# Latent attention heads: one rotation of the shared key part, rotated parts turned in pairs, and two conditioning units moved from TensorE to VectorE

## The chip, the cores and the metric

The kernel runs on one core of a Trainium2 chip. Its engines are TensorE (PE: matrix products and transposes; PEld is its weight load), VectorE (DVE), ScalarE (ACT), GpSimd (POOL) and SyncE (SP, which here issues the large loads). The metric is the device time of one execution in microseconds (us), the median of several runs.

## The reference, cut to what matters

Two transformer blocks and a third, hybrid one run over 256 tokens of width 1024, in 32-bit floats. The change touches the second block's latent attention, and the row of conditioning values that the third block uses later:

```
a = h @ w_a                                  # 384 query latents, 256 key/value latents, 64 shared key values
cq, ckv, k_pe = split(a)
q  = (rms_norm(cq) @ w_qb).reshape(s, 8 heads, 192)
kv = (rms_norm(ckv) @ w_kvb).reshape(s, 8 heads, 128 + 128)
k  = concat([kv[..., :128], broadcast(k_pe over the 8 heads)])
q, k = rms_norm(q, q_gain), rms_norm(k, k_gain)          # over the 192 of a head
q, k = rope(last 64 of q), rope(last 64 of k)
o = causal_softmax(q k^T / sqrt(192)) @ v
mod = silu(c) @ w_ada + b_ada                # 1024 x 6144, in three groups of 2048 columns
```

The block's mixture of experts follows: 64 experts, of which every weight is read (three matrices of 1 MB each).

## The kernel before

Rows of 256 tokens are kept as two tiles of 128 partitions (TT = 2). Weights come in units of 1 MB or less, most into a ring of 12 slots, some into slots that lie in the large work areas A and BC. SyncE issues all these loads in one order, written out by hand; each waits for a semaphore that says that its slot was used. All other engines run one instruction list each, in the order of the stages at the end of the file.

The latent stage: `pa` multiplies the latents, `t3` turns them, `pq` makes the queries (four blocks of two heads), `pkv` the keys and values (four blocks of two heads). ScalarE drains each block (`copy_q`, `copy_kv`) and then squares it (`heads_scalar`), one item of two heads at a time. The items are `l_items`: 0 to 3 hold query heads, 4 to 7 key heads. VectorE takes them in this order (`heads_vector`): it sums the squares (L2118), rotates the last 64 values of each head with four operations, of which two have a wait for their own result behind them (L2124 to L2127), and then scales the item before with the root that GpSimd made of its sum (`heads_gpsimd`, L2092 and L2093; `scale_heads`, L2109 and L2110). The 64 shared key values are copied into all eight key heads first (L2097) and then rotated with each key item. ScalarE's first square waits for these copies.

`t4` turns the heads to have channels on the partitions: 16 fills, in the order `l_order`, four PSUM banks in turn. A fill is one head of queries or keys: two transposes of its 128 plain values and two of its 64 rotated ones (L646). ScalarE evacuates queries and the first two key heads (L658, L660), VectorE the other keys (L662, L664), in the order of the fills; a fill's bank is free for the fill four later once it is evacuated. The rotated channels lie in `peT`, on partitions 0 to 63; partitions 64 to 127 are zeroed by GpSimd (L2177), since scores multiply all 128.

The conditioning row `cond2` has eight units. The first five (`spread` = 5) are added on VectorE with one operation each (L1112, L1115), and TensorE multiplies that sum with ones; the units 5 to 7 it multiplies by themselves, into bank 3 (L1131). These products stand between the fills of `t4` (`latents_tensor`). ScalarE then copies the row and issues its store (L1139, L1141), between its fills 5 and 7. The attention's first scores (L723) and masks (L798) follow; the fills of keys 6 and 7 are evacuated between the first masks.

The next mixture's first loads into A wait for all fills to be evacuated (`rows_turned`), those after them for attention scores (`first_half_2`).

Of the kernel before, what the change touches and what calls it, by code (L numbers as in the profile page):

```python
# [8 lines left out]
ALU = mybir.AluOpType  # L9
# [5 lines left out]
P = 128  # L15
# [91 lines left out]
def build(nc, t, out):  # L107

    with ExitStack() as ctx:
# [514 lines left out]
        def turn_stage(name, ready, jobs, by=None, fill_ready=None, banks=(4, 5), signal="turn_done"):  # L624
# [25 lines left out]
            def evac(eng, scalar, first, last):  # L650
                for f, fill in enumerate(fills):
# [498 lines left out]
        cond1, cond2, cond3 = Conditioning(0, 3), Conditioning(1, 3, 5), Conditioning(2, 3)  # L1150
# [846 lines left out]
        pe_zeroed = shared("cleared", 1)  # L1997
# [13 lines left out]
        def latent_gpsimd(pool):  # L2011
            pool.wait_ge(*pe_zeroed(1))
# [81 lines left out]

        def heads_vector(dve):
            for tt in range(TT):
                nc.vector.tensor_copy(k_l[:, tt, :, NOPE:], hn[:, tt, MLA_Q + MLA_KV:A_WIDTH].unsqueeze(1)  # L2097
                                      .broadcast_to([P, HEADS, ROT])).then_inc(l_pe.sem, 1)
# [6 lines left out]
            def scale_heads(j):  # L2105
                x = l_items[j][0]
# [5 lines left out]
            for j, (x, qk, _) in enumerate(l_items):  # L2112
                dve.wait_ge(*l_sq(j + 1))
                if j == 3:
                    cond2.vector(dve, 1)
                if j >= 2:
                    dve.wait_ge(*l_rs(j - 1))
                nc.vector.tensor_reduce(l_stat(j, 68), l_squares(j).rearrange("p t h d -> p (t h) d"), AX,  # L2118
                                        ALU.add).then_inc(l_ss.sem, 1)
                cs, sn = (gtab[:, qk, k, :, :].unsqueeze(2).broadcast_to([P, TT, n, ROT]) for k in range(2))  # L2120
# [6 lines left out]
                dv.done(nc.vector.tensor_tensor(t1_, t1_, t2_, ALU.add))  # L2127
                if j >= 1:
                    scale_heads(j - 1)
            scale_heads(len(l_items) - 1)  # L2130
# [952 lines left out]
```

## Time and profile before

| | |
|---|---|
| median of 3 runs | 1501.95 us (1501.71 to 1501.95) |
| the profiled execution | 1501.71 us, of which 1500.0 us are the span of the trace |
| TensorE busy | 1301.6 us, 87% of the span |
| VectorE, ScalarE, GpSimd busy | 666.0, 273.8, 131.6 us |
| loads and stores | 513.63 MB, 342 GB/s over the span |

Times in the rows count from the start of the span. The latent stage lies at about 600 to 661 us, its attention at 660 to 696, between the streamed mixtures of the first two blocks. A row of a timeline gives the start, the duration, the engine, the line of the kernel, the operation, the tiles that it writes and reads, the count, and in brackets the time that its engine stood idle before it and what released it. Instructions of an engine overlap at their ends, so the pace of a queue is read from start to start. Matmuls are pipelined and their ends are modelled.

### The profile page before, as it was taken

Reading aid. Unit: us, or ns where it says so; the run is one execution under the profiler, and the core shown is the slowest. Engines: PE = TensorE matmul, PEld = TensorE weight load, DVE = VectorE, ACT = ScalarE, POOL = GpSimd, SP = SyncE. Lnnn points to the kernel's source line nnn. Section 1 sums busy time; section 2 is a strip of 40 time slices with the busy share of each in tenths; the row PEclk is TensorE's granted clock in tenths of the full one; section 3 lists DMA queues with packets and bytes.
Section 4 is the critical chain, followed back from the end, with each engine's and each line's share of the span. In section 5 each row is a group of like instructions: output and inputs, shape, how many; then the busy total and the mean of one; then the engine's idle time right before and its main releaser. Section 6 shows DMA issues by size and latency. Waiting matters only on the chain.

```text
span 1500.0 us, 25645 instructions
## 1 busy us (share of the span) xinstructions
PE 1301.6 (87%) x9730; PEld 806.1 (54%) x9730; DVE 666.0 (44%) x1622; ACT 273.8 (18%) x756; POOL 131.6 (9%) x201
## 2 busy tenths in 40 slices
PE   9999999766776679999999766776679999999997
PEld 4455565433443344665665433443344875899943
DVE  3874634221222123682633221122123646699976
ACT  2153211100010001362211100010000235222200
POOL 1312000000000000210100000000000133222100
PEclk9999999988898899999999898898889999999999
DMA  8979799999999999959899999999999992654400
GB/s 292 401 283 341 289 422 404 421 421 422 422 421 422 422 422 398 365 204 420 321 420 401 421 420 422 422 422 422 423 422 401 384 365 66 211 169 169 169 29 28
DMA packets 120555, 513.63 MB, mean 342 GB/s; under 512 B 12296, under 2 KB 46796, under 8 KB 69144
## 3 DMA queue, kind: packets, MB, share of 16 engines
q1 hardware_dynamic: 118576, 507.30, 84.7%
q0 software_dynamic: 1728, 5.12, 1.0%
q8 instruction: 54, 0.88, 0.2%
q14 instruction: 29, 0.24, 0.0%
q10 hardware_dynamic: 168, 0.09, 0.0%
HBM read 511.39 MB, written 1.08 MB: 342 GB/s over the span
## 4 chain that ended last, share of the span: by engine, by line
PE 58%; DMA 19%; SPq 17%; issue 3%; DVE 2%; ACT 1%; ACTq 0%; POOL 0%; POOLq 0%; DVEq 0%
DMA ring<-in_moe_w_up 15%; SPq L1872 13%; PE bank L1415 9%; PE bank L575 9%; PE bank L2689 8%; PE bank L2724 4%; PE bank L1430 4%; DMA BC<-in_moe_w_up 3%; PE bank L1401 3%; PE bank L1443 3%; PE bank L453 3%; PE bank L2314 3%; PE bank L465 3%; SPq L1881 3%; PE bank L723 2%
## 5 line engine op out<-in xcount | busy, mean ns | idle before, releaser
L1415 PE MATMUL bank<-ring,hT 128*32 128x256 f32 (+1 forms) x2848 | 280.6, 451 | 131.9 <-DMA ring<-in_moe_w_up 65.6
L1415 PEld LDWEIGHTS bank<-ring,hT 128*32 128x32 f32 (+1 forms) x2848 | 147.9, 131 | 233.2 <-issue 170.0
L1707 DVE TENSOR_SCALAR pT<-pT 128x256 f32<-128x256 f32 x34 | 10.0, 294 | 408.1 <-ACT pT L1839 408.1
L1415 PE MATMUL bank<-BC,hT 128*32 128x256 f32 (+1 forms) x1120 | 148.4, 436 | 43.6 <-DMA ring<-in_moe_w_up 22.1
L1401 PEld LDWEIGHTS bank<-gtab,hn 128*128 128x128 f32 x1088 | 129.3, 192 | 15.4 <-issue 14.3
L1401 PE MATMUL bank<-gtab,hn 128*128 128x128 f32 x1088 | 132.5, 275 | 0.1
L1415 PEld LDWEIGHTS bank<-BC,hT 128*32 128x32 f32 (+1 forms) x1120 | 74.8, 127 | 83.5 <-issue 66.5
L1430 PE MATMUL bank<-ring,gtab 128*32 128x512 f32 (+1 forms) x768 | 116.8, 596 | 1.8 <-DMA ring<-in_moe_w_down 1.3
L1443 PE MATMUL bank<-hT,A 128*128 128x512 f32 x256 | 118.3, 605 | 0.0
L575 PE MATMUL bank<-ring,hT 128*128 128x512 f32 (+3 forms) x288 | 99.6, 505 | 0.3 <-DVE hT L314 0.2
L1839 ACT ACTIVATE pT<-bank 128x256 f32<-128x256 f32 x34 | 13.1, 384 | 461.3 <-PE bank L1415 461.3
L279 POOL TENSOR_SCALAR stat<-stat 128x1 f32<-128x1 f32 x12 | 2.8, 235 | 952.0 <-ACT hn L272 951.8
L1648 DVE TENSOR_TENSOR hT<-bank,gains 128x512 f32<-128x512 f32 x34 | 23.5, 691 | 124.7 <-PE bank L1401 124.7
L1443 PEld LDWEIGHTS bank<-hT,A 128*128 128x128 f32 x256 | 46.0, 189 | 59.4 <-issue 59.4
L575 PEld LDWEIGHTS bank<-ring,hT 128*128 128x128 f32 x288 | 51.1, 190 | 46.7 <-issue 44.9
L1828 ACT ACTIVATE hT<-bank,gains 128x128 f32<-128x128 f32 x136 | 38.9, 368 | 162.1 <-PE bank L1401 162.1
L1708 DVE RECIPROCAL pT<-pT 128x256 f32<-128x256 f32 x34 | 59.6, 1753 | 1.2
L1430 PEld LDWEIGHTS bank<-ring,gtab 128*32 128x32 f32 (+1 forms) x768 | 29.4, 112 | 51.6 <-issue 47.2
L1430 PE MATMUL bank<-BC,gtab 128*32 128x512 f32 x224 | 50.8, 595 | 0.0
L1845 ACT ACTIVATE hT<-bank 128x512 f32<-128x512 f32 x34 | 20.3, 597 | 150.6 <-PE bank L1430 150.6
L1761 DVE COPY hT<-bank 128x512 f32<-128x512 f32 x34 | 23.5, 692 | 53.2 <-PE bank L1430 53.2
L1115 DVE SCALAR_TENSOR_TENSOR ring<-ring,small 128x2048 f32<-128x2048 f32 x18 | 42.3, 2351 | 10.2 <-DMA ring<-in_w_ada 8.6
(390 smaller groups left out, 1948.3 us busy)
## 6 DMA issues: line engine op xcount, KB each, us to landing
ring<-in_moe_w_gate SPq DMA_DIRECT2D x90, 1024.0 KB, 25.1
ring<-in_moe_w_up SPq DMA_DIRECT2D x88, 1024.0 KB, 25.5
ring<-in_moe_w_down SPq DMA_DIRECT2D x88, 1024.0 KB, 26.3
BC<-in_moe_w_gate SPq DMA_DIRECT2D x38, 1024.0 KB, 24.7
BC<-in_moe_w_up SPq DMA_DIRECT2D x32, 1024.0 KB, 25.0
BC<-in_moe_w_down SPq DMA_DIRECT2D x28, 1024.0 KB, 26.2
ring<-in_w_ada SPq DMA_DIRECT2D x24, 1024.0 KB, 14.1
ring<-in_w_up SPq DMA_DIRECT2D x22, 1024.0 KB, 7.3
```

The costliest lines, as they stand in the source:

```text
L453: i = nc.tensor.matmul(bank[2 + n][:, :], self.channel(0, c), view(slot(u))[:, c % 4, :], start=(c == 0), stop=(c == DC - 1))
L465: i = nc.tensor.matmul(bank[n][:, :], self.channel(1, c), view(slot(u))[:, c % 4, :], start=(c == 0), stop=(c == DC - 1))
L575: i = nc.tensor.matmul(ps(n, tt)[:, 0:w], lhs(seen + c, tt), view(slot(u))[:, c, :], start=(seen + c == 0), stop=(seen + c == total - 1))
L1401: i = nc.tensor.matmul(TOKENS[half][:, c % 4 * P:(c % 4 + 1) * P], tokens_by_channel[:, tt, c, :], hot[:, tt, :], start=(tt == 0), stop=(t ...
L1415: i = nc.tensor.matmul(GATE[q * cap:(q + 1) * cap, part * FF:(part + 1) * FF], xg[:, c, q * cap:(q + 1) * cap], u[:, c, :], start=(c == 0) ...
L1430: i = nc.tensor.matmul(SIDE[nb][q * cap:(q + 1) * cap, :], hidT[:, c, q * cap:(q + 1) * cap], u[:, c, nb * NB:(nb + 1) * NB], start=(c == ...
L1443: i = nc.tensor.matmul(bank[2 * tt + nb][:, :], share[:, tt * P:(tt + 1) * P], yrow[:, nb * NB:(nb + 1) * NB], start=False, stop=False)
L1708: wait(nc.vector.reciprocal(e, e))
L1872: sp.dma_start(slot(u), expert_src).then_inc(unit_full[s].sem, 16)
L1881: return [sp.value_load(order_i[0:1, bass.ds(place + q, 1)] if i is not None else order_i[0:1, place + q:place + q + 1], min_val=0, max_va ...
L2689: i = nc.tensor.matmul(part_bank(j, k)[:, h * P:(h + 1) * P], weights[h][:, c, :], tokens[:, c, :], start=(c == 0), stop=(c == 3))
L2724: return nc.tensor.matmul(out[:, :], rows, columns, start=(j == 0), stop=(j == PAIRS - 1))
```

## The change

Four edits in the latent stage:

- The shared key part is rotated once, ahead of the copies (`k_rope`, in `pT`); key items are no longer rotated, and their scaling takes the one rotated part for both heads.
- The scaled rotated parts go to an area of their own, two heads side by side (`turned_ropes`, one per item). An even head's fill turns its plain values and the pair's rotated ones; an odd head's fill turns plain values alone. The pair comes out on 128 partitions, and two copies bring the lower 64 to the even head and the upper 64 to the odd head, each on its own partitions. The zeroed halves of `peT` therefore alternate with the head.
- `cond2` has `spread` 7: units 0 to 6 are added on VectorE, and TensorE multiplies the sum and unit 7. VectorE's sums of units 4, 5 and 6 now stand behind the scaling in the items 2, 4 and 6; before, unit 4 was added ahead of item 3.
- TensorE's product of units 4 and 5 ahead of fill 4 is gone; that of units 6 and 7 stays behind fill 5 and waits for the sum of unit 6.

```
-        cond1, cond2, cond3 = Conditioning(0, 3), Conditioning(1, 3, 5), Conditioning(2, 3)
+        cond1, cond2, cond3 = Conditioning(0, 3), Conditioning(1, 3, 7), Conditioning(2, 3)
...
# evac of turn_stage
+                        if isinstance(dst, list):
+                            for (a, b), part in dst:
+                                copy = nc.vector.tensor_copy
+                                i = nc.scalar.activation(part, ps[a:b, :], ACT.Copy) if scalar else copy(part, ps[a:b, :])
+                            continue
...
         def heads_vector(dve):
+            cs, sn = (gtab[:, 1, k, :, :] for k in range(2))
+            nc.vector.tensor_tensor(k_rope, k_rope_in, cs, ALU.mult)
+            nc.vector.tensor_tensor(k_rope_2[:, :, 0:32], k_rope_in[:, :, 32:64], sn[:, :, 0:32], ALU.mult)
+            dv.done(nc.vector.tensor_tensor(k_rope_2[:, :, 32:64], k_rope_in[:, :, 0:32], sn[:, :, 32:64], ALU.mult))
+            dv.done(nc.vector.tensor_tensor(k_rope, k_rope, k_rope_2, ALU.add))
...
             def scale_heads(j):
+                turned = k_rope.unsqueeze(2).broadcast_to([P, TT, n, ROT]) if qk else t1s[j % 2]
                 nc.vector.tensor_tensor(x[:, :, :, 0:NOPE], x[:, :, :, 0:NOPE], r.broadcast_to([P, TT, n, NOPE]), ALU.mult)
-                nc.vector.tensor_tensor(x[:, :, :, NOPE:], t1s[j % 2], r.broadcast_to([P, TT, n, ROT]),
+                nc.vector.tensor_tensor(turned_ropes[j].rearrange("p t (h d) -> p t h d", h=n), turned, r.broadcast_to([P, TT, n, ROT]),
...
             for j, (x, qk, _) in enumerate(l_items):
                 dve.wait_ge(*l_sq(j + 1))
-                if j == 3:
-                    cond2.vector(dve, 1)
...
+                if not qk:
+                    rotate_queries(j)
                 if j >= 1:
                     scale_heads(j - 1)
+                if j in (2, 4, 6):
+                    cond2.vector(dve, 1)
...
-            l_jobs.append((lambda tt, x=x, h=h: x[:, tt, h, 0:NOPE], P, nopeT[:, h, k, :], mla_gain[:, 5 + k:6 + k]))
-            l_jobs.append((lambda tt, x=x, h=h: x[:, tt, h, NOPE:], ROT, peT[0:ROT, h, k, :], None))
+            fill = [(lambda tt, x=x, h=h: x[:, tt, h, 0:NOPE], P, nopeT[:, h, k, :], mla_gain[:, 5 + k:6 + k])]
+            if h % 2 == 0:
+                fill.append((lambda tt, k=k, h=h: turned_ropes[4 * k + h // 2][:, tt, :], P,
+                             [((0, ROT), peT[0:ROT, h, k, :]), ((ROT, P), peT[ROT:P, h + 1, k, :])], None))
+            l_jobs.append(fill)
...
             pe.wait_ge(*pkv.copied(8))
-            cond2.tensor(pe, 4, 6)
             t4.tensor(pe, 4, 6)
             cond2.tensor(pe, 6, 8)
...
-            nc.gpsimd.memset(BC[ROT:P, 16 * S:32 * S], 0.0).then_inc(pe_zeroed.sem, 1)
+            zero = BC[:, 16 * S:32 * S].rearrange("p (h o s) -> p h o s", h=HEADS // 2, o=2)
+            for odd in range(2):
+                nc.gpsimd.memset(zero[ROT * (1 - odd):P - ROT * odd, :, odd, :], 0.0).then_inc(pe_zeroed.sem, 1)
```

## Rows read from the trace of the kernel before

**Rows 1.** The page: span, and shares of the chain that ended last.
```profile
span 1500.0 us, 25645 instructions
...
PE 58%; DMA 19%; SPq 17%; issue 3%; DVE 2%; ACT 1%; ACTq 0%; POOL 0%; POOLq 0%; DVEq 0%
```

**Rows 2.** Windows: length, busy us (count) of PE, PEld, DVE, ACT, POOL; PEclk; DMA share; GB/s.
```profile
650.00:655.00 5.00, 5.00 (x48) 2.21 (x45) 4.86 (x13) 4.92 (x15) 2.87 (x4) 1.00 0.01 3
655.00:660.00 5.00, 4.79 (x45) 4.05 (x38) 4.38 (x11) 3.41 (x10) 0.00 (x0) 1.00 0.02 5
```

**Rows 3.** Timeline of the sync queue: a conditioning unit, the first loads into A.
```profile
623.29 0.33 SPq L253 DMA_DIRECT2D ring<-in_w_ada  x1
...
662.96 0.80 SPq L1872 DMA_DIRECT2D A<-in_moe_w_up  x2
```

**Rows 4.** Chain of waits: start, us, what.
```profile
656.24 1.01 ACTq L1141
...
660.98 0.29 DVE BC L798
```

**Rows 5.** Timeline of TensorE while the heads are turned.
```profile
648.90 1.91 PE L646 MATMUL bank<-konst,A 128*128 128x128 f32 x16
650.74 1.06 PE L1131 MATMUL bank<-ring,konst 128*32 128x512 f32 x8
...
653.62 1.92 PE L1131 MATMUL bank<-ring,small 128*32 128x512 f32 x16
655.48 2.40 PE L646 MATMUL bank<-konst,A 128*128 128x128 f32 x20
```

**Rows 6.** Timeline of VectorE: items 2, 3, 4 and the last.
```profile
633.51 0.95 DVE L2118 TENSOR_REDUCE stat<-hn 128x4 f32<-128x768 f32 x1 [0.58 <-ACT hn L2084]
...
637.38 2.35 DVE L1115 SCALAR_TENSOR_TENSOR ring<-ring,small 128x2048 f32<-128x2048 f32 x1 [0.66 <-ACT hT L2084]
639.65 0.95 DVE L2118 TENSOR_REDUCE stat<-hT 128x4 f32<-128x768 f32 x1
640.51 0.41 DVE L2124 TENSOR_TENSOR hn<-A,gtab 128x256 f32<-128x256 f32 x1
...
641.83 0.69 DVE L2109 TENSOR_TENSOR A<-A,stat 128x512 f32<-128x512 f32 x1
...
642.77 0.95 DVE L2118 TENSOR_REDUCE stat<-hn 128x4 f32<-128x768 f32 x1
...
652.13 0.95 DVE L2118 TENSOR_REDUCE stat<-hT 128x4 f32<-128x768 f32 x1
...
655.25 0.69 DVE L2109 TENSOR_TENSOR A<-A,stat 128x512 f32<-128x512 f32 x1
```

**Rows 7.** Timeline of ScalarE: its first fill.
```profile
651.51 0.46 ACT L658 ACTIVATE BC<-bank,small 128x256 f32<-128x256 f32 x1
651.86 0.36 ACT L660 ACTIVATE BC<-bank 64x256 f32<-64x256 f32 x1
```

**Rows 8.** Timeline of GpSimd: zeroing, latent root, root of the last item.
```profile
601.80 3.51 POOL L2177 MEMSET BC<- 64x4096 f32 x1
616.13 0.19 POOL L2016 TENSOR_SCALAR stat<-stat 128x2 f32<-128x2 f32 x1 [10.82 <-ACT BC L2006]
...
653.54 1.14 POOL L2093 TENSOR_TENSOR stat<-stat 128x4 f32<-128x4 f32 x1
```

**Rows 9.** DMA issues of 622.5 to 624: count, size, us to landing.
```profile
ring<-in_w_ada SPq DMA_DIRECT2D x1, 1024.0 KB, 7.2
```

**Rows 10.** Windows, as in rows 2: an idle stretch and 64 matmuls each.
```profile
835.14:843.40 8.26, 5.31 (x65) 3.29 (x64) 1.86 (x6) 0.60 (x1) 0.00 (x0) 0.79 1.01 420
...
925.94:931.90 5.96, 3.61 (x65) 2.39 (x64) 1.86 (x6) 0.60 (x1) 0.00 (x0) 1.00 1.01 419
```

**Rows 11.** Chain of waits: the mixture's matmuls behind a load.
```profile
1027.71 4.93 PE bank L1415 x64
...
1117.21 6.25 PE bank L1415 x64
```

More of the change, by code:

```diff
@@ L1996, in copy_a @@
             return nc.scalar.activation(hn[:, tt, n * NB:n * NB + ps.shape[1]], ps, ACT.Copy, scale=n2.rstd[:, tt:tt + 1])
-        pe_zeroed = shared("cleared", 1)
+        pe_zeroed = shared("cleared", 2)
         a_sq, a_rs = shared("sum_sq", 4), shared("sum_rs", 2)
@@ L2011, in latent_gpsimd @@
         def latent_gpsimd(pool):
-            pool.wait_ge(*pe_zeroed(1))
+            pool.wait_ge(*pe_zeroed(2))
             for k, (a, b) in enumerate(a_parts):
@@ L2093, in heads_gpsimd @@
                 nc.gpsimd.tensor_tensor(l_stat(j, 84), mean, half[:, 0:TT * L_HEADS], ALU.pow).then_inc(l_rs.sem, 1)
-        def heads_vector(dve):
+        k_rope = pT[:, 0:TT * ROT].rearrange("p (t d) -> p t d", t=TT)
+        k_rope_2 = pT[:, TT * ROT:2 * TT * ROT].rearrange("p (t d) -> p t d", t=TT)
+        k_rope_in = hn[:, :, MLA_Q + MLA_KV:A_WIDTH]
+        turned_ropes = [a.rearrange("p (t d) -> p t d", t=TT) for a in
+                        [l_spare[0][:, 768 + 256 * k:1024 + 256 * k] for k in range(3)] +
+                        [l_spare[1][:, 768 + 256 * k:1024 + 256 * k] for k in range(3)] +
+                        [BC[:, 9728:9984], BC[:, 9984:10240]]]
+        def heads_vector(dve):
+            cs, sn = (gtab[:, 1, k, :, :] for k in range(2))
[3 more added lines that the diff above has]
+            dv.done(nc.vector.tensor_tensor(k_rope, k_rope, k_rope_2, ALU.add))
             for tt in range(TT):
-                nc.vector.tensor_copy(k_l[:, tt, :, NOPE:], hn[:, tt, MLA_Q + MLA_KV:A_WIDTH].unsqueeze(1)
+                nc.vector.tensor_copy(k_l[:, tt, :, NOPE:], k_rope_in[:, tt, :].unsqueeze(1)
                                       .broadcast_to([P, HEADS, ROT])).then_inc(l_pe.sem, 1)
@@ L2127, in heads_vector @@
                 dv.done(nc.vector.tensor_tensor(t1_, t1_, t2_, ALU.add))
+            for j, (x, qk, _) in enumerate(l_items):
+                dve.wait_ge(*l_sq(j + 1))
+                if j >= 2:
+                    dve.wait_ge(*l_rs(j - 1))
+                nc.vector.tensor_reduce(l_stat(j, 68), l_squares(j).rearrange("p t h d -> p (t h) d"), AX,
+                                        ALU.add).then_inc(l_ss.sem, 1)
+                if not qk:
+                    rotate_queries(j)
                 if j >= 1:
                     scale_heads(j - 1)
+                if j in (2, 4, 6):
+                    cond2.vector(dve, 1)
             scale_heads(len(l_items) - 1)
@@ L2176, in rotary_zero_gpsimd @@
             pool.wait_ge(*n2.rooted(TT))
-            nc.gpsimd.memset(BC[ROT:P, 16 * S:32 * S], 0.0).then_inc(pe_zeroed.sem, 1)
+            zero = BC[:, 16 * S:32 * S].rearrange("p (h o s) -> p h o s", h=HEADS // 2, o=2)
+            for odd in range(2):
+                nc.gpsimd.memset(zero[ROT * (1 - odd):P - ROT * odd, :, odd, :], 0.0).then_inc(pe_zeroed.sem, 1)
         def latents_ready(pe):
-            pe.wait_ge(*pe_zeroed(1))
+            pe.wait_ge(*pe_zeroed(2))
         def latent_head(h):
```

12 lines of the change are left out of this document (4 added, 8 removed).

## The prediction

> **What bounds the kernel now.** I began with the profile page: span, and the chain of work that ended last by engine [rows 1]. It alternates between TensorE and the stream of expert weights. The change lies in the second block's latent attention, between two streamed mixtures, so I read the windows of that place next [rows 2]. While the heads are turned, the transfers stand still (0.01 and 0.02 of the DMA engines): the sync queue waits until all heads are turned and issues the next expert weights only then, at 662.96 [rows 3]. So each microsecond that the turning ends earlier moves the following attention, those transfers and the second mixture alike, and nothing downstream holds the gain back; one that is lost moves them the other way. The question is only when the turning ends.
>
> In these windows three engines look full at once: TensorE 5.00 of 5 us, VectorE 4.86, ScalarE 4.92 [rows 2]. The chain of waits names TensorE, then ScalarE's issue of a transfer, then a mask on VectorE at 660.98 [rows 4]. The timelines show why: TensorE turns four fills, multiplies two conditioning units, turns two fills, multiplies two units, turns the rest [rows 5]. VectorE meanwhile runs the last items of the head norm and comes to its own evacuations only after the last scaling, which begins at 655.25 [rows 6]. ScalarE evacuates from 651.51 [rows 7].
>
> **What the change costs and saves: TensorE.** Two units leave it. Two units take 655.48 - 653.62 = 1.86 us [rows 5]. Rotated parts of two heads go through one transpose: 64 transposes become 48. Sixteen take 650.74 - 648.90 = 1.84, so 0.115 each [rows 5], and 16 fewer save 1.84. Together 3.7 us of TensorE. This is not the gain, as the next steps show.
>
> **VectorE.** It gains two sums: one takes 639.65 - 637.38 = 2.27, so +4.54 [rows 6]. It loses four rotations of key items; one lasts from 640.51 to 641.83, 1.32, so -5.28 [rows 6]. It gains one rotation of the shared part, half as wide, ahead of the key copies. No row shows this one; the wide rotation with the same two waits, 1.32, bounds it above, half of that, 0.66, below. I take 1.0, since fixed time and waits do not shrink with the width. Net work: +0.26 (from -0.1 to +0.6). But the old queue stood idle 0.58 and 0.66 for ScalarE's squares ahead of items 2 and 3 [rows 6]; arriving later and with the sum moved from item 3 to item 2, it no longer does: -1.24.
>
> Laying the queue out from these intervals (reduce 0.86, rotation 1.32, scaling 0.94 [rows 6]): item 3 begins at about 639.2 (before 639.65), item 4 at 642.3 (642.77). Items 4 to 7 are then reduce and scaling, 1.8 each, with sums after items 4 and 6. The sum of unit 6 ends at about 652.35, the last reduce runs from 652.3 to 653.2 (before from 652.13). GpSimd's root needs until 654.68 after a reduce that ends at 653.08 [rows 6, 8], 1.6 us. Before, a rotation covered it; now only one scaling does, so the last scaling waits for the root: it starts at 653.2 + 1.6 + 0.05 = 654.85 instead of 655.25. Of the whole exchange on VectorE 0.4 us is left. The added sums wait for their units too: unit 6 is issued at 623.29 and such a load lands in 7.2 us [rows 3, 9], 20 us before its sum.
>
> **The turning itself.** TensorE turns the first four fills with 14 transposes instead of 16 and is through at 650.5. Fill 4 needs the bank of fill 0, which ScalarE begins to empty at 651.51; a scaled copy moves on after 0.35, a plain one takes 0.36 [rows 7]. An even head now has one scaled copy and two plain ones, an odd head one scaled copy alone: 32 copies in all, as before. So the bank is free at 651.86 + 0.72 = 652.6, and TensorE, which filled this time with the two units that left it, stands idle for 2.1 us. Of the 3.7 us these 2.1 are gone. Fills 4 and 5 are through at 653.15, the sum of unit 6 (652.35) is there, two units more: 655.0, against 655.48 before [rows 5]. Behind that stand ScalarE's copy of the row and its transfer issue of 1.01 us [rows 4], so ScalarE's later fills also start 0.45 earlier. The remaining fills have 30 transposes instead of 40, but their banks are emptied by the same number of copies on two engines that start 0.4 to 0.45 earlier; of the 1.15 us I count 0.3. The first mask comes 0.7 earlier. The fill of keys 6 between the first and second mask now has three copies rather than two, which gives back about 0.35 for the second item. I take **0.5 us**, from 0.3 to 0.9. No row shows a copy into the upper 64 partitions: at the time of the 128-partition copy, 0.46 [rows 7], two on the path would cost 0.2 more.
>
> On matmul busy time, the Trainium skill ("Trainium Kernel Development and Optimization", Performance Expectations) says that it is a bad measure because matmuls are pipelined, and takes weight-load time instead. In the same window, weight loads take 2.21 of 5 us where matmuls take 5.00 [rows 2], which agrees. Taking TensorE as the bound there would give the whole 3.7 us; by the rule it would not.
>
> **Edits at no cost.** The zeroing on GpSimd becomes two halves of the same total, 3.51 us; were each as long as the old one, it would still end inside the 10.82 us for which GpSimd then waits [rows 8]. Without that cover the latent roots would come later by the excess. The shared part's rotation delays the first square on ScalarE by 1.0, whose next need of the same queue is later. The slots of units 4 and 5 are freed by sums instead of matmuls, at 646 and 652; they next hold expert weights that are issued after 662 [rows 3], so no transfer changes. Scores of odd heads read the upper half of the zero-padded columns in the same number of matmuls. Behind TensorE's new wait for the sum of unit 6 stand all fills from the seventh on; its slack is 653.15 - 652.35 = 0.8 us.
>
> **Sum.** The profiled execution lasted 1501.71: 1500.0 span [rows 1] and 1.71 around it. It becomes 1501.2. The median lies 0.24 higher, so I predict 1501.4 for the median.
>
> **Rivals.** (1) TensorE is the bound after all: the whole 3.7 us come through, 1498.3. The chain of waits speaks for it, ScalarE's bank of fill 0 and VectorE's last scaling against it. (2) VectorE becomes the bound, slower: if the sum of unit 6 ends later than 653.15, TensorE waits, and with it 10 fills, the row's copy and its issue; the last scaling moves likewise. Two roots of 1.6 that scalings 3 to 6 no longer cover by a rotation, plus the upper bound of the new rotation (+0.3), make it up to 1.9 later than laid out, which after the gain of 0.5 is 1.4 slower: 1503.3; half of it, 1502.4, is its middle. For it speaks that VectorE has no free time from item 4 on; against it, that a scaling and the next reduce (0.94 + 0.86) together just cover a root. (3) TensorE's clock falls in the idle time of 2.1 us. After an idle stretch inside 835.14 to 843.40 the granted clock averaged 0.79 (part of it at 1.2 instead of 2.4 GHz) and the same 64 matmuls kept TensorE busy 5.31 instead of 3.61 us, +1.7; but from 925.94 to 931.90, with 2.35 us idle, it stayed at 1.00 [rows 10]. It would give 1501.4 + 1.7 = 1503.1. The Trainium skill ("TensorE: Matmul & The Clock Gate", Part 1: The HAM clock gate) has it that activity holds the clock up and idleness lets it fall, whatever work follows; by that a new pause is a risk here, and 2.35 us idle at full clock shows that this one is probably too short.
>
> **How the numbers follow.** Forecast 0.68, (2) 0.21, (1) 0.05, (3) 0.06. The measurement of this kernel can tell about 0.2%, 3.0 us. Forecast and (3) and nearly all of (2) lie within it; (1) is faster by more; a pile-up of (2) and (3) slower by more: faster 0.05, same 0.92, slower 0.03. A shift also moves where the second mixture's last matmuls meet the clock's rise: the group of 64 that took 6.25 us at 1117.21 took 4.93 at 1027.71 [rows 11], so up to 1.3 less. The forecast alone is 1500.6 to 1501.7. The range takes in most of (2) above and of this last effect below: 1500.2 to 1502.9.
>
> **What would show it.** In the changed trace: the two conditioning units end near 655.0 and TensorE idles about 2 us after the fourth fill; the last scaling begins near 654.85 after a wait for GpSimd; the first mask at 660.2 to 660.7; the load of the A slots at 662.0 to 662.6; the granted clock 1.00 from 648 to 672. I am wrong if the last scaling comes after 655.3, if TensorE waits for the sum of unit 6, if the first mask comes before 659, or if the time between the mask and the end of the span differs by more than 1.5 us from before.

## The result and the profile after

The changed kernel takes 1507.15 us (median of 7 runs, 1506.18 to 1507.86) against 1501.95 (1501.71 to 1502.70): a ratio of 1.0033, 95% interval 1.0023 to 1.0043. It is 5.2 us slower; 0.5 us faster was predicted, and the time lies outside the range. The profiled execution lasted 1506.18 us, the fastest of the seven, as the 1501.71 is of before's: the two traces differ by 4.5 us, and no trace shows where the other 0.7 us of the medians lie.

The place I had worked out looks nearly as I had laid it out, except for one engine, ScalarE. TensorE after the change, while the heads are turned (start, us, engine, line, operation, in brackets the idle time before it and what ended it; answers to [rows 5]):

```profile
652.59 0.89 PE L646 MATMUL bank<-konst,A 128*128 128x128 f32 x4 [2.12 <-issue]
653.42 1.07 PE L1136 MATMUL bank<-ring,konst 128*32 128x512 f32 x8
...
655.27 0.44 PE L646 MATMUL bank<-konst,A 128*128 128x128 f32 x2
...
657.27 0.44 PE L646 MATMUL bank<-konst,A 128*128 128x128 f32 x2 [0.47 <-DVE BC L660]
...
658.79 0.44 PE L646 MATMUL bank<-konst,A 128*128 128x128 f32 x2 [0.86 <-ACT BC L660]
...
660.66 0.44 PE L646 MATMUL bank<-konst,A 128*128 128x128 f32 x2 [0.35 <-ACT BC L660]
```

It idles 2.12 us ahead of fill 4, and the units end at 655.27 (before 655.48). But then it waits three times, 1.68 us in all, for copies of VectorE and ScalarE that empty its banks. Before, a single 0.2 us wait stood here:

```profile
658.09 2.40 PE L646 MATMUL bank<-konst,A 128*128 128x128 f32 x20 [0.21 <-ACT BC L660]
```

ScalarE after the change (answers to [rows 7] and, with the row's copy L1144 and its store L1146, to [rows 4]):

```profile
651.38 0.46 ACT L663 ACTIVATE BC<-bank,small 128x256 f32<-128x256 f32 x1
651.74 0.76 ACT L660 ACTIVATE BC<-bank 64x256 f32<-64x256 f32 x2
652.52 0.84 ACT L663 ACTIVATE BC<-bank,small 128x256 f32<-128x256 f32 x2
653.25 0.76 ACT L660 ACTIVATE BC<-bank 64x256 f32<-64x256 f32 x2
...
655.92 0.60 ACT L1144 ACTIVATE modrow<-bank 128x512 f32<-128x512 f32 x1
656.55 1.01 ACTq L1146 DMA_DIRECT2D mod_scratch<-modrow  x1
```

A fill of three copies holds it from 651.38 to 652.52, 1.14 us, and two such copies of 64 partitions take 0.78 of that. The row's copy starts at 655.92, later than before, though the units end earlier. Before:

```profile
655.61 0.60 ACT L1139 ACTIVATE modrow<-bank 128x512 f32<-128x512 f32 x1 [0.25 <-PE bank L1131]
```

VectorE after the change (answers to [rows 6] and [rows 4]; L803 is the mask):

```profile
649.89 2.35 DVE L1120 SCALAR_TENSOR_TENSOR ring<-ring,small 128x2048 f32<-128x2048 f32 x1
...
654.93 0.69 DVE L2129 TENSOR_TENSOR A<-A,stat 128x512 f32<-128x512 f32 x1 [0.90 <-POOL stat L2098]
...
661.59 0.29 DVE L803 CUSTOM_DVE_ANT_0 BC<-bank,konst 128x128 f32<-128x128 f32 x1 [1.40 <-PE bank L728]
...
662.20 0.85 DVE L660 COPY BC<-bank 64x256 f32<-64x256 f32 x2
663.08 0.29 DVE L803 CUSTOM_DVE_ANT_0 BC<-bank,konst 128x128 f32<-128x128 f32 x1
```

The last scaling is where it was predicted; the first mask is 0.61 us later than before, the second, with three copies of a fill ahead of it, 1.16. The second mask before:

```profile
661.92 0.28 DVE L798 CUSTOM_DVE_ANT_0 BC<-bank,konst 128x128 f32<-128x128 f32 x1
```

The first load into A follows at 663.80 (before 662.96). At the router behind the attention, by which I mean the first matmul that counts its picks (L1386 before, L1391 after), the kernel is 1.12 us late.

The larger part of the loss is elsewhere. From that matmul to the first matmul of the projection behind the second mixture (L575), before took 446.36 us and after 449.59: +3.23, in a part of the kernel that the diff does not touch. Before, then after:

```profile
720.45 0.43 PE L1386 MATMUL bank<-A,konst 128*128 128x64 f32 x2 [0.44 <-DVE A L1604]
...
1166.81 2.91 PE L575 MATMUL bank<-ring,hT 128*128 128x264 f32 x12 [0.23 <-DVE hT L314]
```

```profile
721.57 0.43 PE L1391 MATMUL bank<-A,konst 128*128 128x64 f32 x2 [0.44 <-DVE A L1609]
...
1171.16 2.91 PE L575 MATMUL bank<-ring,hT 128*128 128x264 f32 x12 [0.22 <-DVE hT L314]
```

From there to the end it is +0.15. 1.12 + 3.23 + 0.15 = 4.50, the difference of the spans (1504.5 and 1500.0). The page's section on DMA queues has the only row that differs much. Of before, then of after (packets, MB, share):

```profile
q8 instruction: 54, 0.88, 0.2%
```

```profile
span 1504.5 us, 25570 instructions
...
q8 instruction: 71, 1.16, 0.3%
```

There are 17 more packets of code, 16 KB each. They fall in the second mixture, whose loop makes three passes of four blocks: nine come from 890 to 1010 and nine from 1010 to 1130, where before has none. DMA queues from 910 to 1030, before (no q8 row), then after:

```profile
q1 hardware_dynamic: 6959, 50.64, 101.4%
```

```profile
q1 hardware_dynamic: 6912, 50.33, 100.9%
q8 instruction: 9, 0.15, 0.5%
```

And of TensorE's waits from the router to the projection, after (us in total, times, longest), a row that before does not have:

```profile
PE bank L1420 <- issue: 3.6, 2, 2.2
```

"Issue" is a wait for nothing that the profile shows: two halts in the loop of the mixture, in the stretch in which code is fetched.

### The profile page after: what moved, and what is told of

Same layout as the page of the kernel before. It is cut to its first block, busy times and chain, and to the rows that moved or that the text cites. A ratio compares the mean times of both kernels' runs of the same rounds, so it can differ in the third digit from the quotient of the medians.

```text
span 1504.5 us, 25570 instructions
## 1 busy us (share of the span) xinstructions
PE 1304.3 (87%) x9698; PEld 805.7 (54%) x9698; DVE 667.0 (44%) x1612; ACT 274.8 (18%) x756; POOL 131.9 (9%) x202
## 3 DMA queue, kind: packets, MB, share of 16 engines
q8 instruction: 71, 1.16, 0.3%
## 4 chain that ended last, share of the span: by engine, by line
PE 34%; DMA 10%; SPq 8%; DVE 2%; issue 1%; ACT 1%; ACTq 0%; POOL 0%; POOLq 0%; DVEq 0%
DMA ring<-in_moe_w_up 9%; PE bank L2718 8%; SPq L1877 6%; PE bank L1420 4%; PE bank L2753 4%; PE bank L2343 3%; PE bank L465 2%; PE bank L453 2%; PE bank L1435 2%; PE bank L1406 2%; PE bank L1448 1%; SPq L1886 1%; PE bank L728 1%; PE bank L2698 1%; DMA ring<-in_moe_w_down 1%
## 5 line engine op out<-in xcount | busy, mean ns | idle before, releaser
L1420 PE MATMUL bank<-ring,hT 128*32 128x256 f32 (+1 forms) x2848 | 285.6, 461 | 140.6 <-DMA ring<-in_moe_w_up 68.8
L575 PE MATMUL bank<-ring,hT 128*128 128x512 f32 (+3 forms) x288 | 99.7, 505 | 0.3 <-DVE hT L314 0.2
L575 PEld LDWEIGHTS bank<-ring,hT 128*128 128x128 f32 x288 | 51.1, 190 | 46.8 <-issue 44.6
L1120 DVE SCALAR_TENSOR_TENSOR ring<-ring,small 128x2048 f32<-128x2048 f32 x20 | 47.0, 2350 | 7.9 <-DMA ring<-in_w_ada 7.0
```

The lines of the kernel that those rows point to most:

```text
L575: i = nc.tensor.matmul(ps(n, tt)[:, 0:w], lhs(seen + c, tt), view(slot(u))[:, c, :], start=(seen + c == 0), stop=(seen + c == total - 1))
L1120: i = nc.vector.scalar_tensor_tensor(out=slot(u), in0=slot(u), scalar=cond_c[:, c:c + 1], in1=slot(self.units[c - 1]), op0=ALU.mult, op1=A ...
L1420: i = nc.tensor.matmul(GATE[q * cap:(q + 1) * cap, part * FF:(part + 1) * FF], xg[:, c, q * cap:(q + 1) * cap], u[:, c, :], start=(c == 0) ...
```

## The experiments

Theory A, formed from these rows: the mixture is a loop that runs from TensorE's code store. The change takes 65 instructions of code out ahead of that loop (64 of them are the 32 matmuls and 32 weight loads that its page has less), so the loop moves, lies over one more block of code, no longer stays in the store, and is fetched again in every pass. The rival: the packets are a symptom, and the mixture is longer because its loads start at other moments.

**Moving the code, first way.** Matmuls that are never executed, in a branch of the first mixture that is not entered; only their place in the code counts. Each matmul is four instructions: the 24 matmuls that after_cut has more, further below, are 96 instructions on its page (25666 against 25570).

```
                with pe.If(over > 0):
+                   if layer == 0:
+                       keep_warm(pe, 7, P, 20)      # after_code_moved; 40 and 10 in before
```

> The changed kernel, with 20 matmuls (80 instructions, 5 KB) added on TensorE in the overflow branch of the first mixture, which is never taken: nothing more is executed, only the code behind it lies 5 KB later, about where it lay before the change (which took 65 instructions, 4.2 KB, out of the code ahead of the second mixture's loop). Theory A (the loop's place among the 16 KB code blocks): the 17 additional code fetches of 860 to 1130 us are gone, the first matmuls of the mixture behind the last late load (1120.24 in the changed kernel, 1117.21 before) come at about 1118, and the time is 1502.6 to 1503.8, with 0.8 to 1.2 us left from the turning of the heads. Theory B (the late turning of the heads moves the stream of loads and costs the whole difference): the time stays at 1507.2.

> The kernel before, with 40 matmuls (160 instructions, 10 KB) in the same branch that is never taken. Nothing of what is executed differs. Theory A: the second mixture's loop now lies over one code block more, fetches of code go on through all of its passes (some 70 packets of code on TensorE's queue in place of 54), and the time rises by 2.5 to 4.5 us, to 1504.5 to 1506.5. Theory B: 1502.0, no difference.

> The kernel before, with 10 matmuls (40 instructions, 2.5 KB) in the same branch. If the place of the code counts only through the number of blocks under the loop (A), this distance leaves that number as it was: 54 packets and 1502.0 us, within 0.4 us. If any shift of the code costs time, it would be 0.5 us or more.

> The changed kernel with the 80 instructions in the branch that is never taken, and ScalarE's copy and store of the conditioning row (0.60 and 1.01 us) moved behind its last fill instead of standing between fills 5 and 7. If ScalarE's late fills hold TensorE (in the changed kernel fill 11 waits 0.86 us and fill 15 waits 0.35 us for its copies), the first mask comes 0.6 to 1.0 us earlier than without the move, at 660.6 to 661.0, and the time is 0.5 to 1.0 below the run with the moved code alone: 1501.8 to 1502.9. If VectorE's fills hold it just as much, the first mask moves by less than 0.3 us.

The last one is after_code_moved with `cond2.scalar(act)` moved behind `t4.scalar(act, 6)`. Measured: 1509.45, 1509.07, 1507.82 and 1509.00 us, all far from what was expected, because the edit has a price of its own. TensorE in after_code_moved, at the end of the first mixture:

```profile
599.14 0.49 PE L1568 MATMUL bank<-konst 128*128 128x128 f32 x2 [4.31 <-issue]
```

The branch over the longer piece of code now ends in a stall of 4.3 to 4.7 us, in all four kernels; neither before nor after has it. So the whole times say nothing here. The packets and the second mixture's length do: 54, 72, 54 and 54 packets, as expected each time, and 446.98, 449.74, 446.28 and 447.03 us from the router to the projection (before 446.36, after 449.59). With the row's store put last it took 69.65 us from fill 4 to the router instead of 68.95 in after_code_moved, but TensorE's granted clock was 0.67 from 660 to 665 there and 1.00 in after_code_moved, so this run doesn't tell.

**Moving the code, second way**: small executed matmuls ahead of the router's counting, where I took TensorE to be idle for 4.7 us.

```
                 keep_warm(pe, 6, NB)
+                if layer == 1:
+                    keep_warm(pe, 6, 8, 17)          # after_padded; 35 in before_padded
```

> After, plus 17 matmuls of 8 columns (68 code instructions) that TensorE executes in its idle time of 4.7 us ahead of the second mixture's picks. They stand behind the never-taken branch and ahead of the second mixture's loop, so the loop lies again almost where it lay before, and no branch is made longer. Theory A (code place): q8 brings 54 packets, from the router's first matmul to the first matmul of the projection behind the mixture 446.3 to 447.0 us (after: 449.6), no idle time of 4 us near 599 us, router at 721.4 to 721.8 as in after, whole time 1502.6 to 1503.6 us. Rival (the packets are a symptom, and the mixture is longer because its loads start at other times): 449.0 to 450.0 us there and 1505.5 to 1507.2 us.

> Before, plus 35 such matmuls (140 code instructions) in the same idle time, nothing else. Theory A: the second mixture's loop crosses into one more block of code: 71 to 73 packets on q8, 449.2 to 450.2 us from the router to the projection (before: 446.4), router at 720.4 to 720.6, whole time 1504.6 to 1505.8 us, though no work is added on the path. Rival: 446.2 to 446.8 us and 1501.8 to 1502.4 us.

> As after_padded, but the rotated parts of a pair are turned in the even head's fill for query pairs 0, 1, 3 and key pairs 0, 2 and in the odd head's fill for query pair 2 and key pairs 1, 3, so that on each bank a fill of three copies is followed by one of one copy. Theory C (the turning is later because fills of three copies follow one another on the same two banks): TensorE's waits of 0.35 to 0.86 us for copies of fills 6, 7 and 11 are gone, first mask at 660.3 to 661.0 (after: 661.6), second mask not over 1.0 us behind it, router at 720.0 to 720.7, whole time 1501.6 to 1502.6 us. Rival D (ScalarE is held by the conditioning row's copy and its store, whichever fill has the three copies): first mask 661.3 or later, router 721.3 or later, and the time of after_padded.

> Before with the conditioning part of the change alone: units 4 and 5 go to VectorE's sum, made after items 2, 4 and 6; rotations and transposes as before. Theory C: the turning's fills are as before, so little of the 1.1 us: last scaling later by the sum less what is idle now, first mask 660.5 to 661.3, router 720.0 to 720.9. Rival D2 (the conditioning part makes the turning late): router 721.2 or later. The code ahead of the second mixture's loop is shorter by 32 instructions: 54 to 57 packets on q8 and 446.2 to 447.0 us there if the loop's start had over 2 KB ahead of it in its block, else 71 packets and 449.5 us.

The idle time was 0.44 us; the rest of that stretch is filled with other matmuls. Each small matmul took 0.22 us and more, and the clock fell under them (0.82 granted from 720 to 726 in before_padded) or right behind them, so the first three whole times (1509.51, 1517.26, 1510.48 us) are again the edit's. Packets and mixture, from the counting matmul on 64x64 to the projection (before 440.71, after 443.94): after_padded 54 and 440.42; before_padded 54 and 440.82, where I had expected over 70, so 140 instructions do not yet reach the next block while 160 did; after_padded_alternate 54 and 441.07. In after_padded_alternate fills of three copies no longer follow one another on a bank. From ScalarE's first copy to the second mask it took 10.66 us, after 11.70, before 10.41; but at the end of the router's logits (the start of L1385) only 0.43 of the 1.25 us were back. TensorE still waited 0.89 and 0.50 us for ScalarE, and the first mask, 661.70, came where rival D has it: by these rows theory C accounts for a third, and the rest is open until the runs below.

before_conditioning_alone (1508.54 us) is the added sums without the cheaper rotations:

```
-        cond1, cond2, cond3 = Conditioning(0, 3), Conditioning(1, 3, 5), Conditioning(2, 3)
+        cond1, cond2, cond3 = Conditioning(0, 3), Conditioning(1, 3, 7), Conditioning(2, 3)
...
+                if j in (2, 4, 6):
+                    cond2.vector(dve, 1)
```

TensorE there:

```profile
656.13 1.06 PE L1131 MATMUL bank<-ring,konst 128*32 128x512 f32 x8 [2.49 <-DVE ring L1115]
```

It waits 2.49 us for VectorE's last sum, and behind the wait its clock falls, which it did not before (windows; columns: length, TensorE busy, granted clock, DMA share, GB/s):

```profile
657.00:659.00 2.00, 2.00 (x13) 0.54 0.00 0
659.00:661.00 2.00, 2.00 (x13) 0.61 0.01 4
```

The first mask comes at 664.68, 3.70 later than before. Of this 2.51 are the later start of these products (656.13 instead of 653.62); the other 1.19 are theirs and the transposes' longer time at the lowered clock. So this is rival (2) of the prediction with rival (3) on top, and what keeps (2) away in the change is the single rotation. I had expected the mask by 661.3 at the latest and was wrong. With 32 instructions less ahead of the loop, there are 71 packets and 443.89 us.

**Moving the code, third way, without any added work**: some matmuls of the second block's output projection are cut into pieces of 128 or 256 columns; the columns stay the same.

```
+                        w = NB // self.cut[1 + n] if 0 < c < DC - 1 else NB
+                        for a in range(0, NB, w):
-                        i = nc.tensor.matmul(bank[n][:, :], self.channel(1, c), view(slot(u))[:, c % 4, :], ...
+                            i = nc.tensor.matmul(bank[n][:, a:a + w], ..., view(slot(u))[:, c % 4, a:a + w], ...
+        o2.cut = (1, 4, 2)                             # after_cut; (2, 4, 4) in before_cut
```

> After, with 12 of the second block's 32 output-projection matmuls of 512 columns cut into four of 128 or two of 256: the same columns, 96 more code instructions behind the never-taken branch and ahead of the second mixture's loop, no added work. Theory A (code place): 54 packets on q8, 440.4 to 441.1 us from the counting matmul on 64x64 to the projection behind the mixture (before 440.7, after 443.9), the turning as in after (router 1.1 us later than before), whole time 1502.8 to 1504.2 us. Rival (the packets are a symptom): 443.5 to 444.2 us there and 1506.0 to 1507.5 us.

> Before, with 24 of these matmuls cut in the same way: 192 more code instructions, no added work. Theory A: the loop crosses into one more block: 71 to 73 packets on q8, 443.6 to 444.3 us from the 64x64 matmul to the projection, router at 720.2 to 720.7 as in before, whole time 1504.6 to 1505.8 us. Rival: 440.4 to 441.1 us and 1501.7 to 1502.5 us.

The page of after_cut, then that of before_cut:

```profile
span 1502.2 us, 25666 instructions
...
q8 instruction: 54, 0.88, 0.2%
```

```profile
span 1506.7 us, 25837 instructions
...
q8 instruction: 72, 1.18, 0.3%
```

after_cut: 1504.08 us (ratio to before 1.0013, interval 1.0004 to 1.0022), mixture 440.61 us: 3.07 us of the loss are back. before_cut: 1506.00 us (1.0025, 1.0016 to 1.0034), mixture 446.32: before becomes 3.9 us slower although nothing of the change is in it. The mixture is 2 us longer than I had expected, in a profiled execution that was the slowest of its kernel (1508.43). Theory A holds in both directions, and the rival falls: with 54 packets the mixture took 440.2 to 441.2 us in the kernels of the second and third way and below, whenever its loads started, and with 71 or 72 it took 443.9 (after, before_conditioning_alone) to 446.3. The cutting itself is not quite free: from the first mask to the router before_cut took 59.95 us, before 59.47.

**What makes the turning late.** All kernels from here on carry the cut of after_cut (54 packets in each); before, before_cut and after stand in the table for comparison. Since runs differ in when the stage begins, the times are counted from ScalarE's first copy of the turning, in us. Each kernel has one trace, but the intervals repeat: the first mask comes at 9.47 in before, before_cut, before_padded and both before kernels with moved code. The cut itself puts the router 0.2 later (after_cut against after).

| kernel | row's copy | first mask | second mask | router |
|---|---|---|---|---|
| before | 4.10 | 9.47 | 10.41 | 68.94 |
| before_cut | 4.10 | 9.47 | 10.41 | 69.42 |
| after | 4.54 | 10.21 | 11.70 | 70.19 |
| after_cut | 4.52 | 10.19 | 11.68 | 70.40 |
| ropes_alone_cut | 4.54 | 10.20 | 11.70 | 70.43 |
| after_cut_interleaved | 4.53 | 10.20 | 11.69 | 70.42 |
| after_cut_low | 3.76 | 9.18 | 10.45 | 69.16 |
| after_cut_q_whole | 4.42 | 10.12 | 11.61 | 70.33 |
| after_cut_store_gpsimd | 4.53 | 9.42 | 10.91 | 69.63 |
| after_cut_mixed_store | 4.01 | 8.71 | 9.65 | 68.38 |

> The rotation and transposes of the change alone, code moved as in after_cut: units 4 and 5 stay on TensorE, VectorE has two sums fewer (4.5 us less). Theory C (the turning's end is set by the copies of ScalarE and VectorE behind the conditioning row, not by VectorE's sums): the two units fill TensorE's idle time of 2.1 us, units end at 655.0 to 655.6, last scaling at 650.5 to 651.5, first mask still at 660.9 to 661.7, whole time that of after_cut within 0.7 us. Rival (VectorE's later end is what costs): first mask 659.0 to 660.3, whole time 1.2 to 2.5 us below after_cut.

It is after with `Conditioning(1, 3, 5)` and the two units back on TensorE. Without VectorE's added sums the masks and the router stay where they are in after_cut; the whole time is 1503.35 us, 0.7 less. The last scaling is at 654.54 rather than at 651, since it waits for ScalarE's squares now, but theory C is right that VectorE's sums are not what costs.

> As after_cut, with the three copies of a fill in another order: one rotated part, the scaled copy, the other rotated part. In the trace of after two rotated copies in a row go on after 0.39 us each on ScalarE and 0.44 on VectorE, in before one moved on after 0.26 and 0.24 to the scaled copy behind it. Theory E1 (two copies of 64 partitions in a row lose the overlap): steps of 0.26 and 0.24 again, row's copy on ScalarE at 655.1 to 655.5 (after: 655.92), first mask at 660.4 to 661.0, whole time 0.6 to 1.2 us below after_cut. E2 (it is the copy into the upper 64 partitions that is slow, wherever it stands): steps of 0.39 or more behind the upper copy only, half of this. E3 (neither): steps and times as in after_cut.

```
-                        if isinstance(dst, list):
+                    if len(copies) == 3:
+                        copies = [copies[1], copies[0], copies[2]]
```

1503.85 us, and the fill takes 1.14 us as in the old order. ScalarE's rows tell which copy it is:

```profile
651.95 0.36 ACT L673 ACTIVATE BC<-bank 64x256 f32<-64x256 f32 x1
652.21 0.46 ACT L671 ACTIVATE BC<-bank,small 128x256 f32<-128x256 f32 x1
652.68 0.38 ACT L673 ACTIVATE BC<-bank 64x256 f32<-64x256 f32 x1
653.09 0.47 ACT L671 ACTIVATE BC<-bank,small 128x256 f32<-128x256 f32 x1
```

The lower half goes on after 0.26 us. The upper half begins only when the copy ahead of it has ended (652.21 + 0.46), and the copy behind it only 0.41 after it. Two in a row are not the cause (E1 falls); the upper half is (E2), but it costs on both of its sides, so reordering gains nothing. The 0.24 that I had given for VectorE is in no row of before; the copy of a key ahead of its second mask starts at 661.59, the mask 0.33 later.

> As after_cut, but the second rotated part of each pair is copied from the lower 64 partitions to the lower 64 (the odd heads' rotated part is thus left out: their scores lack it). Same number and size of copies. Theory E2 (the copy into the upper 64 partitions holds ScalarE longer): a fill of three copies takes ScalarE 0.88 us (0.36 + 2 x 0.26) instead of 1.14, the row's copy starts 0.5 to 0.8 earlier against the first copy (654.9 to 655.6 where the first copy starts at 651.4), 4.0 us from the first copy to the row instead of 4.54. Rival (any third copy costs this): 1.14 and 4.5 us as in after_cut. On VectorE no change by either: 0.40 + 0.44 + 0.44.

```
-        [((0, ROT), peT[0:ROT, h, k, :]), ((ROT, P), peT[ROT:P, h + 1, k, :])]
+        [((0, ROT), peT[0:ROT, h, k, :]), ((0, ROT), peT[0:ROT, h + 1, k, :])]
```

```profile
651.98 0.46 ACT L668 ACTIVATE BC<-bank,small 128x256 f32<-128x256 f32 x1
652.33 0.63 ACT L665 ACTIVATE BC<-bank 64x256 f32<-64x256 f32 x2
652.86 0.82 ACT L668 ACTIVATE BC<-bank,small 128x256 f32<-128x256 f32 x2
...
655.74 0.60 ACT L1149 ACTIVATE modrow<-bank 128x512 f32<-128x512 f32 x1
```

And VectorE's pair of copies between the masks:

```profile
661.77 0.73 DVE L665 COPY BC<-bank 64x256 f32<-64x256 f32 x2
662.43 0.27 DVE L808 CUSTOM_DVE_ANT_0 BC<-bank,konst 128x128 f32<-128x128 f32 x1
```

Same number and size of copies, all in the lower half: 0.88 us instead of 1.14 a fill, the row at 3.76 instead of 4.52, the first mask 1.01 earlier, the second 1.23, the router 1.24. So each copy from and into the upper half costs ScalarE 0.26 us; two in a row on VectorE take 0.66 where they took 0.88 (there I had expected no change). Source and target change their half together in all these kernels, so which of them counts is not shown. The whole time, 1503.89 us, does not resolve this: medians stand up to 2.4 us beside their profiled executions (1506.00 and 1508.43 in before_cut), so for differences of about 1 us I go by the rows.

> As after_cut, but a query pair's rotated part is copied whole, 128 partitions in one copy: only the keys then need zeros in the other half, so ScalarE makes four copies less, all four of them into the upper half. Theory (ScalarE's copies of the turning set its end): from ScalarE's first copy to the row 3.7 to 4.0 us (after_cut 4.52), TensorE's wait for fill 7 shorter by 0.3 to 0.5, first mask 0.6 to 1.2 earlier than in after_cut against the first copy, whole time 1502.8 to 1503.6 us. Rival (VectorE's fills of three copies set it, fill 10 behind fill 6, fill 14 between the masks): first mask at most 0.4 earlier, second mask as far behind it as before, whole time within 0.4 of after_cut.

A query pair is copied whole, and zeros are needed in the keys alone; `fill.append((src, P, peT[:, h, 0, :], None))`. 1502.84 us. In the profiled execution TensorE's clock fell at the units, which then took 2.80 us instead of 1.85, so the masks hide what ScalarE saved: its last copies ahead of the row began 1.0 us earlier than in after_cut and then waited 0.83 us for the units. For the whole copy itself the row is clear: 128 partitions from partition 0 go on after 0.26 us, like 64. The comparison of masks is inconclusive.

> As after_cut, but the conditioning row's store is issued by GpSimd, which has nothing to do then, instead of ScalarE. Theory D (ScalarE held for 1.0 us behind the row delays fill 7): TensorE's waits for fills 7 and 11 (0.85, 0.34) go, first mask 0.6 to 1.0 earlier against ScalarE's first copy, whole time 0.6 to 1.0 us below after_cut. Rival: VectorE's chain of fills 6, 10 and 14 takes over and 0.3 or less is gained.

```
-                act.wait_ge(*self.copied(1))
-                act.dma_start(mod_dram...
+            pool.wait_ge(*cond2.copied(1))
+            cond2.store(pool)
```

1503.96 us, 0.1 less than after_cut, so the whole time does not show the 0.6 to 1.0 that I had expected. In the rows, masks and router come 0.77 us earlier than in after_cut, TensorE's waits for ScalarE (0.85 and 0.34) are gone, and waits of 0.65 and 0.47 for VectorE's fills 6 and 10 are what is left. By the rows this is theory D, in the middle of what it expected.

> As after_cut, with the store on GpSimd and one part of each pair copied whole: queries for pairs 0 and 2, keys for pairs 1 and 3. Fill 14 between the masks has two copies, fill 6 two, fills 3 and 11 three. If the turning's 1.1 us is ScalarE's upper copies, its issue and the three copies of fill 14, all of it comes back and some of the saved work with it: first mask 1.4 to 2.2 earlier than in after_cut against the first copy, second mask 0.9 behind the first, whole time 1500.8 to 1502.0 us, below before. Rival (TensorE's clock falls or VectorE's last scaling sets the end): less than 1.0 us, 1503 us or more.

The store on GpSimd, and one part of each pair copied whole: `whole_part(h)` is 0 (queries) for pairs 0 and 2, 1 (keys) for pairs 1 and 3. 1502.37 us, a ratio to before of 1.0000 (0.9991 to 1.0009). VectorE's masks:

```profile
660.97 0.29 DVE L808 CUSTOM_DVE_ANT_0 BC<-bank,konst 128x128 f32<-128x128 f32 x1 [0.90 <-PE bank L733]
...
661.91 0.28 DVE L808 CUSTOM_DVE_ANT_0 BC<-bank,konst 128x128 f32<-128x128 f32 x1
```

From the first copy they come 1.48 and 2.03 us earlier than in after_cut, and the router 0.56 earlier than in before itself. Against after_cut_store_gpsimd, from which it differs by the whole copies alone, the router is 1.25 earlier. By the rows all that the turning had lost is back and some of the saved work with it, 0.2 us for the cut matmuls already paid. The whole time does not show it: I had expected 1500.8 to 1502.0, and the median is that of before. It is the best form of the change that I have; it beats after by 4.8 us, and before by nothing that can be measured.

## Why the prediction was wrong

**Right.** TensorE's 3.7 us of work are gone and give no gain, 2.12 us idle (2.1 predicted), fill 4 at 652.59 (652.6), units' end 655.27 (655.0), sum of unit 6 over at 652.24 (652.35), the wait for GpSimd's root ahead of the last scaling, that scaling at 654.93 (654.85); the rotation of the shared part took 0.91 us from 624.43 (1.0 taken). The clock stayed at 1.00 in the profiled execution. VectorE's exchange was thus sized rightly, and before_conditioning_alone shows that it had to be: without the cheaper rotations TensorE's last products start 2.5 us later.

**Wrong: the copies of the turning** (0.5 us gain predicted, 1.12 lost at the router). The step that failed is "the same number of copies on two engines that start 0.4 to 0.45 earlier". I saw that no row showed a copy into the upper 64 partitions, and bounded it by the time of the 128-partition copy, two on the path, 0.2 us. What matters is not how long such a copy lasts (0.38 us, the lower one 0.36) but that it overlaps with neither neighbour: 0.26 us each on ScalarE, 0.22 on VectorE. Five stand on ScalarE, three of them ahead of the row's copy: 3 x 0.26 = 0.78, and the row came at 4.54 instead of 3.76. So ScalarE's later fills started 0.3 later than before instead of 0.45 earlier, and TensorE waited for them. The fill between the masks was priced at 0.35 for its third copy; the second mask is 1.49 behind the first instead of 0.94, 0.55 more. My 0.72 for the two plain copies of the first fill was right only by accident (0.78): I took the duration of a copy, 0.36, where the row behind it showed that the next one begins after less.

Without these copies the 0.5 us would not have come either. after_cut_low has none of them, and the row's copy is 0.34 us earlier than in before, the first mask 0.29 instead of 0.7, and the second 0.04 later; the router, less 0.2 for the cut, is where it was. TensorE still waits 0.53 us for VectorE and 0.18 for ScalarE there: VectorE begins its fills 0.2 earlier than in before and frees the bank of fill 6, which now has three copies instead of two, 0.1 later. "Of the 1.15 us I count 0.3" counted the copies and not which fill they stand in; this is read from the rows and not tested.

The Trainium skill ("VectorE: DVE Perf Modes", Two Vector instructions with no wait between them) has this rule for VectorE: an instruction with an input or output that starts in another group of 32 partitions than that of the last instruction on the same memory is held until every earlier one has finished. VectorE's pair of 0.88 against 0.66 us agrees. ScalarE's rows above show the same there.

**Wrong: "nothing downstream holds the gain back; one that is lost moves them the other way".** The stages behind the turning did not only shift: the mixture became 3.23 us longer. I counted instructions as work and never as code with a place. The row of q8 was on the page, and its split over windows shows that none came in the mixture from 910 to 1030: a loop that stays loaded, and so can cease to. No rival held this, and the range, made from the turning alone, could not. The point that I set for being wrong did catch it: from the first mask to the end of the span it is 839.0 us before and 842.9 after.

The position can be read from the runs together. Instructions added ahead of the loop, relative to before (counted in the program), and packets: -65: 71, -32: 71; 0, 3, 15, 31, 40, 63, 140: 54; 160 and 192: 72. The Trainium skill ("Runtime: NRT & Kernel Launch", Instruction fetch mechanics) says that code is fetched in blocks of 256 instructions, 16 KiB, and that TensorE's store holds 128 KiB. The runs agree: 0.88 MB in 54 packets is 16 KB each, and -65 and -32 are 191 and 224 of a round of 256, beside 160 and 192. The same section calls the crossing of a block mostly hidden; here a loop over one block more costs 3.2 us and up. That the loop just fits, and what it would need to fit, is argued from this and not shown. How the two halts of 3.6 us in sum become 3.2 at the mixture's end was not taken apart either, and the sum of halts does not give the loss: before_conditioning_alone halts 12.0 us in three and its mixture is 3.2 longer than before's, before_cut 9.7 us in three and 5.6.

**The rivals.** (1) did not happen, (2) not in the change. The price of (2), up to 1.9 us, does not follow from its terms as written (two roots of 1.6 and 0.3 are 3.5); nothing here hung on it. (3), the clock falling in TensorE's new idle time, did not happen in the profiled execution of after but does happen in others of its family. Windows from 653 to 657, after, then after_padded, where TensorE had idled 2.12 and 2.13 us (columns as in [rows 2]):

```profile
653.00:657.00 4.00, 3.75 (x31) 1.91 (x30) 3.08 (x8) 3.44 (x9) 1.63 (x2) 1.00 0.00 0
```

```profile
653.00:657.00 4.00, 3.96 (x23) 1.29 (x23) 2.36 (x5) 3.66 (x10) 1.90 (x2) 0.70 0.00 0
```

With 0.70 granted, part of it at 1.2 instead of 2.4 GHz, the units end 0.9 us later and the first mask comes 0.43 later, both counted from ScalarE's first copy. It fell in three of the eleven profiled executions with this idle stretch of 1.7 to 2.1 us (after_padded, after_cut_q_whole, after_code_moved_row_last); so the 2.35 us idle at full clock of [rows 10] did not show that the pause was too short. I had given this 1.7 us and a chance of 0.06: the price was too high and the chance too low.

## What to carry to other kernels

A change that only removes instructions moves all the code behind them: where the packets of code show that a loop is fetched once and then stays, its place is a resource, and the sum needs a term, and the range a case, for a loop that no longer stays. Price an operation by the distance from its start to the next one's start in rows of the same kind, never by its duration, and for a copy on other partitions than its neighbours' assume that it overlaps with nothing until a row shows that it does. Work taken off an engine that waits anyway is worth nothing, while work moved onto the engine that hands its buffers back decides the stage; here four whole copies in place of eight half ones were worth 1.25 us, and the sixteen transposes nothing that the rows show.

## What the runs showed of the hardware

A loop of TensorE whose code moves by 32 instructions can be fetched anew in every pass: 9 packets in each 120 us instead of none, and 3.2 us in 440 (5.6 in before_cut's profiled execution), though code is 0.15 of 50 MB moved there. A taken branch over a piece of code made longer by 40 to 160 instructions stalled TensorE for 4.3 to 4.7 us where it had not stalled at all. A copy from partitions 64 to 127 to the same partitions, between copies that start at partition 0, costs 0.26 us more on ScalarE and 0.22 on VectorE, and a copy of 128 partitions from 0 costs ScalarE no more than one of 64 (0.26 to the next start). And behind an idle stretch of 1.7 to 2.1 us on TensorE the granted clock fell in some executions (0.70 in after_padded) and not in others (1.00 in after).
